# A two-block transformer step on one core: first transfers on one queue, first weights by quarters, eleven unread products in place of 28

## The chip, the cores and the metric

The kernel runs on one core of one Trainium2 chip. The metric is the device time of one execution in microseconds (us); lower is better. PE is TensorE, DVE is VectorE, ACT is ScalarE, POOL is GpSimd, SP is SyncE.

## The reference, cut to what matters

The reference takes 256 tokens of width 1024 (float32) through two blocks, each of two layers, with several kinds of attention, feed-forward parts and mixtures of experts. The very first step is the projection of the input `x` by the weights of the even mixer. The change touches how `x` and those weights come into the core, and the first products on them.

```python
def even_mixer(x, rel_bias, w_in, conv_w, a_log, dt_bias, norm_w, w_out):
    bsz, seq, _ = x.shape                 # 1, 256, width 1024
    q_a, k_a, v_a, z_a, b_a, a_a, q_b, k_b, v_b = jnp.split(x @ w_in, EVEN_SPLITS, axis=-1)
    ...
    o_b = dilated_attention(q_b.reshape(shp), k_b.reshape(shp), v_b.reshape(shp), rel_bias).astype(x.dtype)
    return jnp.concatenate([o_a, o_b], axis=-1) @ w_out
```

## The kernel before

Each engine has its own program, and waits on semaphores tie them together. `wait_ge` on an engine holds everything behind it on that engine, its DMA issues too. The work is an order written out by hand. Weights come in slots of 128 partitions x 4096 float32 (2 MB), by a list `LOADS`, into three slots (`ring`) that SP fills; SP waits for a slot's last reader (`used`) before it issues the next load into it. The list begins with `("we", 6)`, `("we", 7)`, `("we", 8)`, `("wev",)`, `("wev2",)`.

At the start two engines issue DMAs. SP issues all of `("we", 6)` in one DMA and then waits for `PAR`, the landing of three parameter transfers (`cp`, the rest of `kc`, `rp`), before `("we", 7)`. ACT issues, in this order, `x` half 0, the identity matrix `ident` (64 KB), `x` half 1, `cp`, the rest of `kc`, `rp`, and then begins its part of `even()`:

```python
for h in range(2):
    a.dma_start(x[:, h, :], ...).then_inc(s_x[h], 16)
    if h == 0:
        a.dma_start(ident, ins["kc"][:, 0:128]).then_inc(s_x[0], 16)
a.dma_start(cp[:, :], ins["cp"]).then_inc(s_par, 16)
```

PE (`even()` in `tensor`, line 925) first does 28 products on a tile of ones whose result nobody reads (`warm(28, ones)`). A float32 product shows in the trace as two MATMUL records. Then comes `first_tiles(0, ("we", 6), "qb")`, line 708. It transposes half 0 of `x` (`turn_x(0, 0)`: eight transposes into two PSUM banks, `kp` = 0 and 1), waits for all of `("we", 6)`, and multiplies. `part(c, h, kp)` is four products: column tile `c` (of 4), token half `h`, and four of the eight blocks of the inner dimension (`kp`). All four tiles of (h 0, kp 0) come first, then (h 0, kp 1) with the transposes of half 1 in the middle of them, then those of h 1: 64 products in all. The transposed `x` is copied out of PSUM into `xTs` by DVE for kp 0 and by ACT for kp 1 (`x_transposed`, lines 1577 and 2509); `ready(h, kp)` waits for that copy. After the first tiles PE waits for `PAR`, makes the product `hrow` and goes on with `("we", 7)` and `("we", 8)` in `proj_T`. DVE empties the four banks of the first tiles.

The weights lie in memory with the four column tiles side by side (`tiles`): element [k, c, n] at `512 k + 128 c + n` of a partition's row. For some weights (`NARROW`) the host lays them out tile by tile (`by_tile`): [c, k, n].

Of the kernel before, what the change touches and what calls it, by code (L numbers as in the profile page):

```python
# [215 lines left out]
CHUNKS = {4: SB_CH, 6: RET_CH}  # L216

NARROW = ("ws", "wso", "wr", "wrv", "wro")
LEVELS = (0, 1, 2, 4, 8, 16, 32, 64)


# [24 lines left out]
LOADS = all_loads()  # L246
# [41 lines left out]
PLACE = all_slots()  # L288
# [84 lines left out]
def emit(nc, ctx, ins, out):  # L373
# [8 lines left out]
    def sem(name):  # L382
        return ctx.enter_context(nc.semaphore(name))
# [22 lines left out]
    kc = sb("kc_sb", ncon)  # L406
# [20 lines left out]
    s_pe, s_dve, s_act, s_pool = sem("pe_done"), sem("dve_done"), sem("act_done"), sem("pool_done")  # L427

    s_x = [sem(f"x{h}_landed") for h in range(2)]
    s_par = sem("params_landed")  # L430
    s_ring = [sem(f"ring{i}_landed") for i in range(WIDE)]
    s_more = [sem(f"second{i}_landed") for i in range(WIDE)]
# [230 lines left out]
    def tensor():  # L663
# [44 lines left out]
        def first_tiles(n, src, tag, xT=xT):  # L708


            if src[0] in NARROW:
                view = slot(src, 32).rearrange("p (c k) n -> p k c n", c=4)
            else:
                view = slot(src, 8).rearrange("p k (c n) -> p k c n", c=4)

            def part(c, h, kp):
                tk = slice(h * 128, h * 128 + 128)
                for k in range(4 * kp, 4 * kp + 4):
                    r = mm(banks[c][:, tk], view[:, k, c, :], xT[:, k, tk], k == 0, k == 7)
                return r  # L720

            def ready(h, kp):
                t.wait_ge(*(v if kp == 0 and (n == 0 or h) else a)("xT", n, h, kp))

            turn_x(n, 0)
            if src[0] in NARROW:
                for h in range(2):
                    t.wait_ge(*half_arrived(src, h))
            else:
                t.wait_ge(*arrived(src))  # L730
            banks = [bank(tag, c) for c in range(4)]
            ready(0, 0)
            for c in range(4):
                part(c, 0, 0)
            ready(0, 1)
            for c in range(2):
                part(c, 0, 1)
            turn_x(n, 1)
            for c in range(2, 4):
                part(c, 0, 1)  # L740
            ready(1, 0)
            for c in range(4):
                part(c, 1, 0)
            ready(1, 1)
            for c in range(4):
                part(c, 1, 1).then_inc(s_pe, t.did(tag, c))
            t.note("used", src)

        def proj_T(src, tag, n, c, last):
            view = slot(src, 8)  # L750
            if c == 0:
                t.wait_ge(*arrived(src))
            b = bank(tag, n)
            for k in range(8):
                r = mm(b[:, 0:256], view[:, k, c * 128:c * 128 + 128], xT[:, k, :], k == 0, k == 7)
            r.then_inc(s_pe, t.did(tag, n))
            if c == last:
                t.note("used", src)
# [165 lines left out]

        def even():
            t.wait_ge(*g("ones"))
            warm(28, ones[:, :])
            first_tiles(0, ("we", 6), "qb")
            t.wait_ge(*PAR)
            t.wait_ge(*g("consts"))  # L930
# [1561 lines left out]
    def scalar():  # L2492
# [537 lines left out]
            tables("natural_log_exp_and_others")  # L3030
            a.note("pre", 6)

        for h in range(2):
            a.dma_start(x[:, h, :], ins["x"][h * 128:h * 128 + 128, :]).then_inc(s_x[h], 16)
            if h == 0:
                a.dma_start(ident, ins["kc"][:, 0:128]).then_inc(s_x[0], 16)
        a.dma_start(cp[:, :], ins["cp"]).then_inc(s_par, 16)
        a.dma_start(kc[:, 128:ncon], ins["kc"][:, 128:ncon]).then_inc(s_par, 16)
        a.dma_start(rp[:, :], ins["rp"].broadcast_to([128, nrow])).then_inc(s_par, 16)
# [167 lines left out]
    def sync():  # L3207
        def load_expert(name, src, h):

            i, _, old = PLACE[name]  # L3210
            lo = 2048 * h
            if i < SLOTS:
                dst = ring[:, i * 4096 + lo:i * 4096 + lo + 2048]
            else:
                dst = M[name[1]].ringx[:, (i - SLOTS) * 4096 + lo:(i - SLOTS) * 4096 + lo + 2048]
            if i >= SLOTS and (old is None or old[1] != name[1]) and i not in ABOVE[name[1]]:


                s.wait_ge(*(v("sbo", 15) if not name[1] else t("used", ("wro", 3)) if i == 3 else v("unit", 7)))
            elif i >= SLOTS and old is None:  # L3220

                for lane in (t, v, a, g):
                    s.wait_ge(*lane("pre", 3))
            elif old[0] in EXPERT:
                s.wait_ge(*t("used", old, h))
            else:
                s.wait_ge(*t("used", old))
            s.dma_start(dst, src[:, lo:lo + 2048]).then_inc((s_more if h else s_ring)[i], 16)

        def load_experts(names, src):  # L3230
            for h in range(2):
                for name in names:
                    load_expert(name, src(name), h)

        def last_used(name):

            return [p for p in LOADS[:LOADS.index(name)] if PLACE[p][0] == PLACE[name][0] and not (p[0] in ("mg", "mu", "md") and p[2] > 16)][-1]


        HEAD = (("wr", 0), ("wr", 1))  # L3240

        def load(name, src, old=None):
            i = PLACE[name][0]
            old = old or PLACE[name][2]
            if name[0] in NARROW:
                for h in range(2):
                    if old in FIRST:
                        n, first = FIRST[old]
                        s.wait_ge(*t("part", n, first + 2 * h + 1))
                    else:  # L3250
                        s.wait_ge(*(t("used", old) if ("used", old) in t.at else v("used", old)))
                    lo = 2048 * h
                    s.dma_start(ring[:, i * 4096 + lo:i * 4096 + lo + 2048], src[:, lo:lo + 2048]).then_inc(s_half[2 * i + h], 16)
                return
            if old is not None:
                s.wait_ge(*(t("used", old) if ("used", old) in t.at else v("used", old)))
            s.dma_start(ring[:, i * 4096:i * 4096 + width(name)], src).then_inc(s_ring[i], 16)

        def chosen(name):
            return ins[name[0]][bass.ds(ids[name[2] - 16] + name[1] * 16, 1)].rearrange("a p n -> (a p) n")  # L3260

        for place, name in enumerate(LOADS):
            if place == 1:
                s.wait_ge(*PAR)
            if name in HEAD:
                continue
            if name[0] not in EXPERT:
                load(name, source(name))
                continue
            if name[2] < 16:  # L3270

                before, behind = LOADS[place - 1], LOADS[place + 1]
                if name[2] % 2 and before == (name[0], name[1], name[2] - 1):
                    continue
                load_experts([name] + [behind] * (name[2] % 2 == 0 and behind == (name[0], name[1], name[2] + 1)), source)
                continue
            if name[0] != "mg" or name[2] not in (16, 17):
                continue
            l = name[1]
            n, m = 5 + 2 * l, M[l]  # L3280
            if name[2] == 16:
                s.wait_ge(*v("eids", n, 0))
                ids = [s.e.value_load(m.eids[0:1, 0:1], min_val=0, max_val=15)]
                for w in EXPERT:
                    load_experts([(w, l, 16)], chosen)
                continue
            s.wait_ge(*v("eids", n, 6))
            ids += [s.e.value_load(m.eids[0:1, j:j + 1], min_val=0, max_val=15) for j in range(1, 7)]
            flag = s.e.value_load(m.eids[0:1, 7:8], min_val=0, max_val=1)
            seen, rest = dict(s.seen), moe_loads(l, 9, 12)  # L3290
            with s.e.If(flag > 0):
                for i in range(0, len(rest), 2):
                    load_experts(rest[i:i + 2], chosen)
                if l == 0:
                    for name in HEAD:
                        load(name, source(name))
            with s.e.Else():
                for i in range(WIDE):
                    mine = [PLACE[name][1] for name in rest if PLACE[name][0] == i]
                    s.e.wait_ge(s_ring[i], 16 * (mine[0] - 1))  # L3300
                    s.e.sem_inc(s_ring[i], 16 * len(mine))
                    s.e.wait_ge(s_more[i], 16 * (SECOND[[name for name in rest if PLACE[name][0] == i][0]] - 1))
                    s.e.sem_inc(s_more[i], 16 * len(mine))
                s.seen = dict(seen)
                if l == 0:

                    for name in HEAD:
                        load(name, source(name), last_used(name))
            s.seen = seen
# [128 lines left out]
```

## Time and profile before

| | us |
|---|---|
| median of 3 runs | 1819.53 |
| lowest and highest | 1815.80 and 1820.54 |
| the profiled execution, its own time | 1823.21 |
| its span | 1821.5 |
| its mean granted TensorE clock | 0.982 of full |

PE is busy for 1736.7 us of the span (95%), DVE for 976.5 us, ACT for 641.2 us, POOL for 230.2 us; the DMA engines move 443.05 MB, 243 GB/s in the mean. All times in the rows further down are from that profiled execution, counted from the start of the span. A row of the timeline merges instructions of one kind; a bracket behind it tells how long the engine sat idle before and what ended that.

### The profile page before, as it was taken

Reading aid. Unit: us, or ns where it says so; the run is one execution under the profiler, and the core shown is the slowest. Engines: PE = TensorE matmul, PEld = TensorE weight load, DVE = VectorE, ACT = ScalarE, POOL = GpSimd, SP = SyncE. Lnnn points to the kernel's source line nnn. Section 1 sums busy time; section 2 is a strip of 40 time slices with the busy share of each in tenths; the row PEclk is TensorE's granted clock in tenths of the full one; section 3 lists DMA queues with packets and bytes.
Section 4 is the critical chain, followed back from the end, with each engine's and each line's share of the span. In section 5 each row is a group of like instructions: output and inputs, shape, how many; then the busy total and the mean of one; then the engine's idle time right before and its main releaser. Section 6 shows DMA issues by size and latency. Waiting matters only on the chain. (4 is left out here: it accounts for less than half of the span.)

```text
span 1821.5 us, 25863 instructions
## 1 busy us (share of the span) xinstructions
PE 1736.7 (95%) x10464; PEld 1280.2 (70%) x10464; DVE 976.5 (54%) x1806; ACT 641.2 (35%) x1078; POOL 230.2 (13%) x217
## 2 busy tenths in 40 slices
PE   9999999999999989999999989999899999899987
PEld 8788875799886544999888764434489898544434
DVE  1176664688541575787456663233267867533223
ACT  1025322467430224666446431111144455311111
POOL 0000000163110130353002302000000200010000
PEclk9899999999999889999999999999999999999999
DMA  8422186445434595455344659999934555799995
GB/s 306 149 94 93 60 339 249 185 181 213 162 139 162 185 362 232 161 213 187 139 144 177 247 202 420 420 420 420 371 121 160 185 208 208 308 419 420 420 420 230
DMA packets 51853, 443.05 MB, mean 243 GB/s; under 512 B 5900, under 2 KB 6160, under 8 KB 9104
## 3 DMA queue, kind: packets, MB, share of 16 engines
q1 hardware_dynamic: 47664, 426.79, 60.1%
q0 software_dynamic: 2480, 8.92, 1.3%
q10 hardware_dynamic: 1584, 5.61, 0.8%
q8 instruction: 86, 1.41, 0.3%
q14 instruction: 39, 0.32, 0.0%
HBM read 440.25 MB, written 1.05 MB: 242 GB/s over the span
## 5 line engine op out<-in xcount | busy, mean ns | idle before, releaser
L88 ACT ACTIVATE arena<-ps 128x384 f32<-128x384 f32 (+5 forms) x233 | 101.6, 436 | 546.3 <-PE ps L82 344.1
L82 PE MATMUL ps<-ringx,arena 128*64 128x512 f32 x1056 | 276.2, 594 | 7.9 <-DMA ringx<-in_mg 3.5
L82 PE MATMUL ps<-xsplit_f,wsplit_f 128*128 128x256 f32 x2112 | 257.1, 284 | 3.5 <-ACT xsplit_f L88 2.7
L82 PEld LDWEIGHTS ps<-xsplit_f,wsplit_f 128*128 128x128 f32 x2112 | 255.5, 193 | 5.5 <-ACT xsplit_f L88 4.2
L82 PE MATMUL ps<-ring,arena 128*64 128x512 f32 (+1 forms) x704 | 228.8, 598 | 9.5 <-DMA ring<-in_mu 6.0
L91 DVE TENSOR_TENSOR wsplit_f<-ring,wsplit_f 128x1024 fp32r<-128x1024 f32 x132 | 180.6, 1372 | 70.4 <-ACT wsplit_f L88 70.4
L82 PEld LDWEIGHTS ps<-ringx,arena 128*64 128x64 f32 x1056 | 89.6, 137 | 170.3 <-issue 156.3
L82 PE MATMUL ps<-xTs,ring 128*128 128x256 f32 (+1 forms) x960 | 188.3, 356 | 2.3 <-ACT xTs L88 1.8
L82 PEld LDWEIGHTS ps<-xTs,ring 128*128 128x128 f32 x960 | 163.0, 193 | 24.5 <-issue 6.6
L88 ACT ACTIVATE wsplit_f<-ring 128x1024 fp32r<-128x1024 f32 x132 | 138.2, 1051 | 57.5 <-PE ps L82 56.5
L82 PEld LDWEIGHTS ps<-ring,arena 128*64 128x64 f32 (+1 forms) x704 | 78.6, 148 | 104.8 <-issue 89.2
L91 DVE TENSOR_TENSOR ringlo<-ring,ringhi 128x1024 fp32r<-128x1024 f32 x88 | 120.7, 1387 | 58.1 <-ACT ringhi L88 57.7
L82 PE MATMUL ps<-arena 128*128 128x128 f32 (+5 forms) x1128 | 142.2, 306 | 4.2 <-DVE arena L91 2.0
L91 POOL TENSOR_TENSOR small<-small,half 128x1 f32<-128x1 f32 x16 | 9.3, 583 | 1031.3 <-DVE small L95 1029.7
L82 PEld LDWEIGHTS ps<-arena 128*128 128x128 f32 (+2 forms) x1128 | 127.5, 192 | 16.5 <-DVE arena L91 4.0
L99 DVE SCALAR_TENSOR_TENSOR arena<-ps,cp_sb,arena 128x255 f32<-128x255 f32 (+2 forms) x230 | 110.9, 482 | 45.7 <-ACT arena L88 34.2
L91 DVE TENSOR_TENSOR arena<-arena,ps 128x384 f32<-128x384 f32 (+2 forms) x74 | 42.9, 579 | 165.6 <-PE ps L82 152.8
L82 PE MATMUL ps<-wsplit_f,gsplit 128*128 128x512 f32 x528 | 120.1, 389 | 0.0
L82 PEld LDWEIGHTS ps<-wsplit_f,gsplit 128*128 128x128 f32 x528 | 99.0, 188 | 20.5
L88 ACT ACTIVATE ringhi<-ring 128x1024 fp32r<-128x1024 f32 x88 | 91.7, 1052 | 52.9 <-PE ps L82 45.2
L91 POOL TENSOR_TENSOR arena<-arena 128x256 f32<-128x256 f32 (+1 forms) x58 | 78.3, 1350 | 196.4 <-DVE arena L91 110.3
L82 PE MATMUL ps<-xth,ringhi 128*128 128x256 f32 x320 | 94.9, 296 | 2.2 <-DVE ringlo L91 1.7
(197 smaller groups left out, 2425.0 us busy)
## 6 DMA issues: line engine op xcount, KB each, us to landing
ring<-in_ada SPq DMA_DIRECT2D x24, 2048.0 KB, 8.0
ring<-in_wu SPq DMA_DIRECT2D x22, 2048.0 KB, 8.1
ringx<-in_mg SPq DMA_DIRECT2D x44, 1024.0 KB, 20.8
ringx<-in_mu SPq DMA_DIRECT2D x44, 1024.0 KB, 23.8
ringx<-in_md SPq DMA_DIRECT2D x44, 1024.0 KB, 26.1
ring<-in_md SPq DMA_DIRECT2D x24, 1024.0 KB, 25.5
ring<-in_mg SPq DMA_DIRECT2D x24, 1024.0 KB, 20.7
ring<-in_mu SPq DMA_DIRECT2D x24, 1024.0 KB, 23.9
```

Of the source, the lines that this page charges most:

```text
L82: return self.e.matmul(o, l, r, start=start, stop=stop, skip_group_check=True)
L88: return self.e.activation(o, i, f, **k)
L91: return self.e.tensor_tensor(o, a, b, op)
L99: return self.e.scalar_tensor_tensor(out=o, in0=a, scalar=s, in1=b, op0=op0, op1=op1)
```

## The change

Four things change. (1) SP issues `x` half 0, `ident`, quarter 0 of `("we", 6)`, `x` half 1 and the quarters 1 to 3, each quarter (512 KB, one column tile) with a semaphore of its own. It then issues `("we", 7)` at once, and waits for `PAR` before `("we", 8)`. (2) ACT issues nothing until half 1 of `x` has landed; then it issues `cp`, `kc` and `rp`. (3) The 28 unread products become 11, and three more follow the transposes of half 0. (4) For n = 0, `first_tiles` goes tile by tile: tiles 0 and 1 for half 0 (both kp), each as its quarter lands, with the transposes of half 1 between them; then half 1 of each tile, tiles 2 and 3 with both halves. The host lays out all `we` weights tile by tile, and `proj_T` reads them so; the number and the shapes of products are the same.

```diff
@@ first_tiles @@
-            if src[0] in NARROW:
+            if src[0] in BY_TILE:                    # BY_TILE = NARROW + ("we",)
                 view = slot(src, 32).rearrange("p (c k) n -> p k c n", c=4)
...
-            else:
+            elif n:
                 t.wait_ge(*arrived(src))
+            if n == 0:
+                warm(3, ones[:, :])
             banks = [bank(tag, c) for c in range(4)]
+            if n == 0:
+                for c in range(2):
+                    t.wait_ge(s_tile[c], 16)
+                    for kp in range(2):
+                        ready(0, kp)
+                        part(c, 0, kp)
+                    if c == 0:
+                        turn_x(n, 1)
+                for c in range(4):
+                    if c >= 2:
+                        t.wait_ge(*((s_tile[c], 16) if c < 3 else arrived(src)))
+                        part(c, 0, 0)
+                        part(c, 0, 1)
+                    for kp in range(2):
+                        ready(1, kp)
+                        r = part(c, 1, kp)
+                    r.then_inc(s_pe, t.did(tag, c))
+                t.note("used", src)
+                return
@@ proj_T @@
-            view = slot(src, 8)
+            if src[0] in BY_TILE:
+                view = slot(src, 32)[:, 8 * c:8 * c + 8, :]
+            else:
+                view = slot(src, 8)[:, :, c * 128:c * 128 + 128]
...
-                r = mm(b[:, 0:256], view[:, k, c * 128:c * 128 + 128], xT[:, k, :], k == 0, k == 7)
+                r = mm(b[:, 0:256], view[:, k, :], xT[:, k, :], k == 0, k == 7)
@@ even (PE) @@
-            warm(28, ones[:, :])
+            warm(11, ones[:, :])
@@ scalar @@
-        for h in range(2):
-            a.dma_start(x[:, h, :], ins["x"][h * 128:h * 128 + 128, :]).then_inc(s_x[h], 16)
-            if h == 0:
-                a.dma_start(ident, ins["kc"][:, 0:128]).then_inc(s_x[0], 16)
+        a.wait_ge(s_x[1], 16)
         a.dma_start(cp[:, :], ins["cp"]).then_inc(s_par, 16)
@@ sync @@
+        def load_x(h):
+            s.dma_start(x[:, h, :], ins["x"][h * 128:h * 128 + 128, :]).then_inc(s_x[h], 16)
+
+        def load_first(c):
+            lo, name = 1024 * c, LOADS[0]
+            s.dma_start(slot(name, 1)[:, 0, lo:lo + 1024], source(name)[:, lo:lo + 1024]) \
+                .then_inc(s_tile[c] if c < 3 else s_ring[PLACE[name][0]], 16)
+
+        load_x(0)
+        s.dma_start(ident, ins["kc"][:, 0:128]).then_inc(s_x[0], 16)
+        load_first(0)
+        load_x(1)
+        for c in range(1, 4):
+            load_first(c)
         for place, name in enumerate(LOADS):
-            if place == 1:
+            if place == 0:
+                continue
+            if place == 2:
                 s.wait_ge(*PAR)
```

## Rows read from the trace of the kernel before

**Rows 1.** The page of the profile: its span.
```profile
span 1821.5 us, 25863 instructions
```

**Rows 2.** The timeline, 0 to 28 us: start, length, engine, line, operation, count, idle before.
```profile
...
1.07 7.99 PE L82 MATMUL ps<-ones 128*128 128x128 f32 x56 [1.07 <-POOL ones L114]
...
2.23 0.53 ACTq L117 DMA_DIRECT2D cp_sb<-in_cp  x1
...
3.28 0.49 ACTq L117 DMA_DIRECT2D rp_sb<-in_rp  x1
...
10.75 1.09 PE L85 MATMUL ps<-kc_sb,xs 128*128 128x128 f32 x8 [1.69 <-DMA kc_sb<-in_kc]
11.45 0.69 DVE L102 COPY xTs<-ps 128x512 f32<-128x512 f32 x1 [10.12 <-PE ps L85]
11.93 1.28 ACT L88 ACT_TABLE_LOAD   x1 [11.93 <-PE ps L85]
...
12.28 5.60 PE L82 MATMUL ps<-xTs,ring 128*128 128x128 f32 x48 [0.44 <-DVE xTs L102]
13.23 0.60 ACT L88 ACTIVATE xTs<-ps 128x512 f32<-128x512 f32 x1
...
17.72 1.04 PE L85 MATMUL ps<-kc_sb,xs 128*128 128x128 f32 x8
...
18.59 9.10 PE L82 MATMUL ps<-xTs,ring 128*128 128x128 f32 x80
...
27.62 0.81 PE L82 MATMUL ps<-kc_sb,cp_sb 32*4 32x384 f32 x2
```

**Rows 3.** The timeline from 16 us, the DMA queue of SP.
```profile
...
17.30 0.82 SPq L117 DMA_DIRECT2D ring<-in_we  x2
```

**Rows 4.** Windows from the start and one later: busy times, PEclk, DMA share, GB/s.
```profile
...
0.00:4.10 4.10, 3.03 (x14) 3.03 (x15) 0.24 (x4) 0.00 (x0) 0.60 (x7) 1.00 0.51 133
...
0.00:6.70 6.70, 5.63 (x37) 5.63 (x38) 0.24 (x4) 0.00 (x0) 0.60 (x7) 1.00 0.72 251
0.00:16.00 16.00, 12.80 (x97) 12.41 (x98) 0.93 (x5) 1.88 (x2) 0.60 (x7) 1.00 0.87 342
20.00:24.00 4.00, 4.00 (x38) 4.00 (x38) 0.00 (x0) 2.18 (x3) 0.00 (x0) 1.00 0.94 401
```

**Rows 5.** DMA view, 0 to 8 us: GB/s in 40 slices of 0.2 us, then queues.
```profile
...
GB/s 0 0 0 0 0 0 0 0 0 492 573 82 0 82 20 82 348 369 492 123 307 696 532 123 369 881 266 102 410 860 266 123 451 799 266 143 676 717 184 123
...
q1 hardware_dynamic: 109, 1.79, 61.3%
q10 hardware_dynamic: 99, 0.41, 13.9%
```

**Rows 6.** Windows around waits of PE: PE busy (instructions), PEclk, DMA share, GB/s.
```profile
...
79.30:92.90 13.60, 13.60 (x44) 0.50 0.30 127
...
528.40:530.40 2.00, 0.16 (x2) 1.00 0.00 0
...
666.70:670.80 4.10, 0.38 (x8) 0.88 1.02 436
670.80:676.60 5.80, 5.45 (x30) 0.50 0.98 414
1316.10:1318.80 2.70, 0.18 (x2) 0.91 0.99 413
1318.80:1321.70 2.90, 2.90 (x7) 0.50 0.10 34
1325.90:1329.20 3.30, 0.10 (x2) 0.90 0.64 257
1329.20:1332.00 2.80, 2.80 (x13) 0.50 0.01 3
```

**Rows 7.** Groups of instructions on PE, 1 to 4 us: busy, mean ns.
```profile
...
L82 PE MATMUL ps<-ones 128*128 128x128 f32 x13 | 3.1, 433 | 1.1 <-POOL ones L114 1.1
```

**Rows 8.** The same groups, 5 to 8 us.
```profile
...
L82 PE MATMUL ps<-ones 128*128 128x128 f32 x29 | 3.4, 275 | 0.0
```

More of the change, by code:

```diff
@@ L218 @@
 NARROW = ("ws", "wso", "wr", "wrv", "wro")
+BY_TILE = NARROW + ("we",)
 LEVELS = (0, 1, 2, 4, 8, 16, 32, 64)
@@ L429, in emit @@
     s_x = [sem(f"x{h}_landed") for h in range(2)]
+    s_tile = [sem(f"first_tile{c}_landed") for c in range(3)]
     s_par = sem("params_landed")
@@ L3372 @@
     ins = {"x": a["x"][0]}
-    ins["we"] = tiles(_np.concatenate([we[:, 0:3072], we[:, 3084:4620]], 1), 8, 512)
+    even_tiles = tiles(_np.concatenate([we[:, 0:3072], we[:, 3084:4620]], 1), 8, 512)
     ins["wev"] = tiles(we[:, 4620:5132], 8, 512)
@@ L3390, in by_tile @@
         return w.reshape(-1, 128, 8, 4, 128).transpose(0, 1, 3, 2, 4).reshape(w.shape)
+    ins["we"] = by_tile(even_tiles)
     ws = a["sb_w_in_2"][0]
```

## The prediction

> **What bounds the kernel now.** I read the page first: the kernel is long, with a span of 1821.5 us [rows 1], and PE is busy for nearly all of it. So what the first 28 us save or lose on PE is carried through to the end: every later load waits for a slot that PE frees, and so moves along with PE. The timeline of the first 28 us comes next [rows 2]. The reader is to see a chain there. PE's 28 unread products run from 1.07 to 9.06. Then PE waits 1.69 us for the `x` half 0 and the identity, and starts the transposes at 10.75. DVE's copy of the first bank ends at 12.14, and the products on `("we", 6)` start at 12.28. ACT's copy of the second bank is ready at 13.83 (13.23 and 0.60), but the 16 products of kp 0 hide it. From 12.28 on PE has no idle time until `hrow` at 27.62. So the start is bound by the landing of `x`, then by PE. SP issues the next weights only at 17.30, when the last parameter transfer has landed [rows 3]; the windows and the DMA view tell how the bytes come in [rows 4, 5]. Last, I looked for what a wait of PE does to its clock [rows 6 to 8].
>
> The sum is made on the moment at which `hrow` starts, 27.62 in the profiled execution (span 1821.5 us, own time 1823.21 us). The median of the runs, 1819.53 us, is 3.7 us below that own time; I subtract the same difference from both.
>
> **When the first bytes land.** All bytes of the start (x 1.05 MB, identity 0.07, `("we", 6)` 2.10, parameters 2.27: 5.4 MB with roundings) are moved by 16.0 (342 GB/s x 16.0 us = 5.5 MB) [rows 4], and SP's wait for the last of them ends at 17.30 [rows 3]. So a landing comes some 1.3 us behind its last byte. After the change the order is one queue's. x half 0 and the identity are 590 KB; 545 KB are moved by 4.1 us (133 x 4.1) and 1682 KB by 6.7 us (251 x 6.7) [rows 4]. So 590 KB are there at 4.2 and land at 5.5. Quarter 0 makes it 1114 KB, at 5.4, landing 6.7. x half 1 makes it 1638 KB, at 6.6, landing 7.9. In the first 8 us two queues shared evenly by packets, 109 to 99, which is why 16 KB packets of weights held back the 4 KB packets of `x`; per byte both kinds took the same (61.3% of 16 x 8 us for 1.79 MB, 13.9% for 0.41 MB: 23 GB/s of an engine each) [rows 5]. So smaller packets cost nothing here.
>
> **PE until the wait.** Eleven unread products are 22 records. By 4.0 us 13 had run at 433 ns each, later ones have 275 ns [rows 7, 8], so the 22 end at about 5.0, before `x` lands: removing 17 products costs nothing and removes nothing from the path. Transposes 5.5 to 6.6 (1.09). DVE's copy is ready at 5.5 + 0.70 (10.75 to 11.45) + 0.69 = 6.9. The three new products (6 records at 9.10/80 = 0.114 us) end at 7.2 and cover that copy. part(0, 0, 0), eight records, ends at 8.1 [rows 2].
>
> **The new wait.** Now PE needs ACT's copy of kp 1. ACT waits for half 1 of `x` (7.9), and three issues are queued behind that wait: before, they took from 2.23 to 3.28 + 0.49 = 3.77, so 1.54 us. Only then does it come to the table load and the copy, 11.93 to 13.83, so 1.90 us [rows 2]. The table load began only after the transposes, so it sits behind that wait and isn't done ahead. The copy is ready at 7.9 + 1.54 + 1.90 = 11.3, and PE goes on at 11.4. PE idles for 3.3 us where before it had 12 more products of kp 0 to do.
>
> The row shows the copy starting 1.30 us after the load began, with nothing behind the load. The Trainium skill (ScalarE: Activation LUTs, What ACT_TABLE_LOAD costs) puts 1.38 us of drain beside a load of 1.28 us; by it the copy would be ready 1.4 us later and the forecast 1.4 us higher. I go by the row.
>
> **The rest of the first tiles.** 60 products are 120 records x 0.114 = 13.65 us, the transposes of half 1 put 18.59 - 17.72 = 0.87 us among them [rows 2]. 11.4 + 13.65 + 0.87 = 25.9, against 27.62: a gain of 1.7 us. Quarters 1 to 3 are 3.2 MB with all before them. Even if `cp` takes half of the bandwidth from 8.9 on, quarter 1 is there by 11 and quarter 3 by 18, and they are needed after 13 and after 21. Their waits cost nothing. The other layout leaves shape and count of all products alone: 0. `("we", 7)` goes earlier, which nothing needs, and can only delay the parameters: 5.47 MB were moved by 16.0, the 2.0 MB left over take 5.0 us at 401 GB/s [rows 4], so all parameters land by 22.3, 3.6 us before PE asks for them. `("we", 8)`, 5 us later than before, is needed some 12 us after `hrow`: hidden.
>
> **The clock.** Three other waits show what follows. Over 4.1 us with 0.38 us of work, over 2.7 and over 3.3 us, the granted clock fell in each, and PE went on at 0.50, the lower level of 1.2 GHz, for 5.8, 2.9 and 2.8 us. A wait of 2.0 us at 528 left it at 1.00 [rows 6]. The new wait of 3.3 us is like the three. A stretch at half speed costs half of its length: 2.9, 1.5 or 1.4 us, 1.9 in the mean, and the bounds are 0 and that of the longest low stretch shown, 13.6 us at 79.3 [rows 6], 6.8 us. I take 1.9, by the three nearest rows. (If the clock has not yet risen at 5 us with fewer unread products, the loss up to 11.4 lies in the wait, and what comes after is the same price.)
>
> Sum: -1.7 + 1.9 = +0.2 us. Median 1819.7 us; profiled execution 1823.4, span 1821.7.
>
> **The rivals.**
> (a) The clock holds over the wait. Then the gain of 1.7 us stays: 1817.8. For it: the wait at 528 [rows 6], and that PE has 0.9 us of products right before. Against it: three of three at 2.7 us and more.
> (b) The bytes come sooner on one queue. From 2.2 to 3.0 us nearly nothing moved [rows 5]; without that dip all landings are 0.8 us earlier, the copy is ready at 10.5 and the end is 25.1: 2.5 us gained before the clock's price, 1818.9 with it, 1817.0 without. The Trainium skill (DMA: Bandwidth & Descriptors, Anatomy of one DMA) gives, for the software path, a fixed 2.0 us and 436 GB/s; by that estimate x half 1 would be there at 6.6. The rows here speak for 7.9.
> (c) ACT isn't late, because the table load or the issues lie beside the wait after all. Then products run without a stop from 7.2: 7.2 + 128 x 0.114 + 0.87 = 22.6, just after the parameters' 22.3. That is 5.0 us gained, 1814.5, and the most that this change can give. Against it: the table load at 11.93 came 0.09 us behind the transposes, not at the start [rows 2].
> (d) The other side: the clock stays low through most of the first tiles. From 3.4 us at the lower level on, the kernel is slower than before; at 13.6 us, as at 79.3 [rows 6], it loses 6.8 - 1.7 = 5.1 us: 1824.6; beyond 14.4 us it is slower by 0.3%. Against it: with the same products the clock held all the way from 12.28 before, and the three stretches after waits were 5.8 us at most.
> (e) The change moves nothing at all, as the end of the first tiles stays within 0.5 us of 27.6: that is the forecast's own result, by two terms that cancel, and the trace tells them apart.
>
> **How the numbers follow.** Forecast 0.57, with its own range 1818.3 to 1821.2 (price of the clock 1.4 to 2.9, landings by 0.8 us sooner or 0.5 later). (a) and (b) 0.28 together, (c) 0.09, (d) 0.06. A change under 0.3% (5.5 us) can't be told from none here: the three runs of before lie 4.7 us apart. Only (c) with luck, or (d) with more than its row, gets past it: faster 0.03, slower 0.03, the same 0.94. The range leaves out (d) and most of (c) and takes in the scatter of a median of a few runs, some 1.5 us: 1815.5 to 1822.5.
>
> **What would show it.** In the profile after: transposes at about 5.5; a wait of PE for ACT's `xTs` copy of about 3.3 us, ending near 11.4; ACT's issues at 7.9 to 9.4 and its table load right behind; MATMUL records of some 433 ns in place of 275 after that wait for 3 to 6 us; `hrow` near 27.8; `("we", 7)` issued before 5 us. The forecast is wrong if PE doesn't wait for ACT, if x half 1 lands before 7 us or after 9 us, if the records after the wait keep 275 ns, or if PE waits for parameters at `hrow`.

## The result, and the profile after

| | us |
|---|---|
| before, median of 10 runs | 1818.95 (1815.80 to 1823.61) |
| after, median of 10 runs | 1825.95 (1821.16 to 1827.46) |
| ratio | 1.0032, interval 1.0019 to 1.0045 |
| profiled execution after | 1826.19, span 1824.5 |

The change makes the kernel slower by 0.32%, some 6 us (the two medians themselves lie 7.0 us apart). The forecast was 1819.7 with a range up to 1822.5: the time lies 3.5 us above it.

The timeline of the changed kernel from the start (start, length, engine, line, what, count, idle before); it answers to [rows 2, 3]:

```profile
0.81 0.39 SPq L117 DMA_DIRECT2D xs<-in_x  x1
...
5.93 1.70 PE L85 MATMUL ps<-kc_sb,xs 128*128 128x128 f32 x8
...
8.23 1.16 PE L82 MATMUL ps<-xTs,ring 128*128 128x128 f32 x8
9.51 0.38 ACTq L117 DMA_DIRECT2D cp_sb<-in_cp  x1
9.93 0.45 ACTq L117 DMA_DIRECT2D kc_sb<-in_kc  x1
10.40 0.45 ACTq L117 DMA_DIRECT2D rp_sb<-in_rp  x1
10.95 1.28 ACT L88 ACT_TABLE_LOAD   x1 [10.95 <-issue]
12.24 0.60 ACT L88 ACTIVATE xTs<-ps 128x512 f32<-128x512 f32 x1
...
12.89 1.16 PE L82 MATMUL ps<-xTs,ring 128*128 128x128 f32 x8 [3.51 <-ACT xTs L88]
...
13.89 1.70 PE L85 MATMUL ps<-kc_sb,xs 128*128 128x128 f32 x8
...
15.38 13.69 PE L82 MATMUL ps<-xTs,ring 128*128 128x128 f32 x112
...
24.19 0.21 ACT L88 ACTIVATE small<-cp_sb 128x8 f32<-128x8 f32 x1 [6.67 <-DMA rp_sb<-in_rp]
...
29.00 0.80 PE L82 MATMUL ps<-kc_sb,cp_sb 32*4 32x384 f32 x2
```

The reader sees the forecast chain, link by link: `x` half 1 lands at 9.5 and releases ACT's issues; then comes the table load, then the copy, which ends at 12.84, and PE has waited 3.51 us. Behind it the transposes take 1.70 us in place of 1.04. `hrow` starts at 29.00, 1.4 us later than before [rows 2].

Windows of the changed kernel (PE, PEld, DVE, ACT, POOL busy, then granted clock, DMA share, GB/s), to compare with [rows 4, 6]:

```profile
0.00:6.70 6.70, 5.63 (x26) 5.63 (x27) 0.24 (x4) 0.00 (x0) 0.60 (x7) 1.00 0.69 195
...
12.80:17.50 4.70, 4.61 (x26) 4.61 (x27) 0.69 (x1) 1.90 (x3) 0.00 (x0) 0.64 0.98 414
```

After the wait the granted clock is 0.64 in the mean up to 17.5 us. By 6.7 us only 1.31 MB are there (195 x 6.7) and not 1.68. The DMA queues from 0 to 8 us (packets, MB, share of 16 engines):

```profile
q1 hardware_dynamic: 574, 1.66, 71.2%
```

But 1.4 us at `hrow` are not 3.0 us in the span, nor 6 in the median. Farther on the two profiles run together again: the first product on the output weights starts at 300.01 after and at 299.57 before. The rest appears at one place. The timeline of PE in the changed kernel there:

```profile
682.84 0.22 PE L82 MATMUL ps<-tmpn,gate 128*32 128x4 f32 x8
686.26 3.44 PE L82 MATMUL ps<-ring,gate 128*32 128x512 f32 x16 [3.20 <-DMA ring<-in_ada]
689.46 0.31 PE L82 MATMUL ps<-tmpn,gate 128*32 128x4 f32 x8
689.70 2.09 PE L82 MATMUL ps<-arena,ones 128*128 128x512 f32 x4
```

And in the kernel before:

```profile
683.00 0.22 PE L82 MATMUL ps<-tmpn,gate 128*32 128x4 f32 x8
685.05 1.92 PE L82 MATMUL ps<-ring,gate 128*32 128x512 f32 x16 [1.83 <-DMA ring<-in_ada]
686.79 0.22 PE L82 MATMUL ps<-tmpn,gate 128*32 128x4 f32 x8
```

PE comes to the same load at the same time (within 0.2 us), waits 3.20 us in place of 1.83, and then runs 16 records in 3.44 us in place of 1.92: the clock has fallen after the longer wait (granted 0.57 in the mean from 686 to 690 us). The next step begins at 689.70 against 686.94. Most of these 2.8 us stay: the spans end 3.0 us apart. So there were two losses: one at the start, which the forecast had, and one at 683 us, which it had not. The DMA view of the moment at which SP issues that load, 677 us, first before (677.2 to 678.0), with its time to landing:

```profile
q8 instruction: 1, 0.02, 8.3%
...
ring<-in_ada SPq DMA_DIRECT2D x1, 2048.0 KB, 7.6
```

and after (677.0 to 678.0, and the queues at 683.2 to 684.8):

```profile
ring<-in_ada SPq DMA_DIRECT2D x1, 2048.0 KB, 9.0
...
q1 hardware_dynamic: 57, 0.69, 102.7%
q8 instruction: 1, 0.02, 3.7%
```

The same 2 MB take 9.0 us in place of 7.6. A packet of the instruction queue (16 KB, 0.95 us) starts at 683.7 after, 6.5 us behind the load's issue and just as its last bytes come in; before, it started at 677.3, with the issue. A load raises its semaphore in 16 steps. After, the trace has 15 of them 7.4 us behind the issue and the last alone at 9.0; before, 15 were in by 7.5 and the last came at 7.6. So one sixteenth of the load is late, and the rest is not.

### The profile page after: what moved, and what is told of

Its sections match the earlier page's. It is cut to its first block and busy times, and to the rows that moved or that the text cites. A ratio compares the mean times of both kernels' runs of the same rounds, so it can differ in the third digit from the quotient of the medians.

```text
span 1824.5 us, 25810 instructions
## 1 busy us (share of the span) xinstructions
PE 1736.2 (95%) x10436; PEld 1280.3 (70%) x10436; DVE 976.6 (54%) x1806; ACT 641.1 (35%) x1078; POOL 229.5 (13%) x217
```

## The experiments

Each time is a median; each ratio is against the kernel before, measured alongside, with a 95% interval. Theory 1: the loss is ACT's late copy and the low clock behind it. Theory 2: the layout or the early load costs farther on. Theory 3, formed on the first profiles: the length of PE's program ahead of a place sets where the instruction packets fall among the loads. The change takes 14 products out of that program; the trace has 28 matmul and 28 weight-load instructions of PE less for them, 56 in all. Theory 4: chance.

**The changed kernel again.** No edit.

> The changed kernel once more, unaltered, for a second profile. In the first one hrow starts at 29.00 us, 1.4 us later than before, and 1.6 us more come at 683 us, where PE waits for an ada load and its clock then falls. Theory 1 (the loss is ACT's late copy and the low clock after it, and what lies behind it is the luck of the clock): hrow again at 28 to 31, the wait of 3.5 us again, median 1822 to 1827, and the place of the later differences need not be the same. Theory 2 (something else in the change, the layout of the weights or the early load, costs further on): the same 1.6 us again at 683 us.

1824.96 us, ratio 1.0022 (1.0009 to 1.0035). `hrow` at 29.04 after a wait of 3.48 us; at 682 us a wait of 3.50 us, and the clock falls again. Both losses come back. Theory 4 would have the second one come and go.

**ACT copies first.**

```diff
 def x_transposed(...):                  # scalar
     for h in range(2):
+        if h and n == 0:
+            load_params()                # a.wait_ge(s_x[1], 16) and the three issues
```

> ACT copies half 0 of x before it waits for half 1 and issues the parameters; all else as in the changed kernel. Theory 1: no wait of PE for ACT of over 1 us, no low clock in the first tiles; their 64 products run from 8.2 to about 23.7, hrow waits for the parameters until about 24.5; so 4.5 us under the changed kernel and 2 to 3 us under the kernel before, 1814 to 1818. Theory 2 (the loss lies in the layout or behind the start): still 1822 or more.

1819.42 us, ratio 0.9988 (0.9974 to 1.0002). Its timeline of the start:

```profile
9.02 0.60 ACT L88 ACTIVATE xTs<-ps 128x512 f32<-128x512 f32 x1
9.50 0.38 ACTq L117 DMA_DIRECT2D cp_sb<-in_cp  x1
...
9.67 1.16 PE L82 MATMUL ps<-xTs,ring 128*128 128x128 f32 x8 [0.29 <-ACT xTs L88]
...
11.54 12.67 PE L82 MATMUL ps<-xTs,ring 128*128 128x128 f32 x112
...
25.29 0.80 PE L82 MATMUL ps<-kc_sb,cp_sb 32*4 32x384 f32 x2 [1.08 <-DMA rp_sb<-in_rp]
```

The wait is 0.29 us, 112 records take 12.67 us in place of 13.69, and `hrow`, now held by the parameters, starts 3.7 us earlier than in the changed kernel. The start is won, 2.3 us under before; the wait at 680 us is 3.44 us with a fall of the clock, as in the changed kernel. The ratio is 2.2 us under before (4.7 under to 0.4 over), as expected (2 to 3 us); the expected 1814 to 1818 itself was missed, as the kernel before stood at 1820.89 here. By the profile 2.3 us won and 2.8 lost should leave 0.5 us over, at the edge of the interval: in this time the second loss doesn't show.

**Unread products in the wait.**

```diff
+                        if (c, kp) == (0, 1):
+                            warm(15, ones[:, :])
                         ready(0, kp)
```

> 15 unread products are put into PE's wait for ACT's copy; the wait itself stays as long. Theory 1: MATMUL records after it keep 275 ns, first tiles end 1.7 us earlier than in the changed kernel, hrow at 27.3; median 1.5 to 3 us lower, 1822 to 1824. If the clock at the start has no price: no change, hrow at 29.0.

1819.09 us, ratio 0.9996 (0.9983 to 1.001). Its timeline of PE at the start:

```profile
8.37 3.51 PE L82 MATMUL ps<-ones 128*128 128x128 f32 x30
12.05 1.16 PE L82 MATMUL ps<-xTs,ring 128*128 128x128 f32 x8 [0.17 <-ACT xTs L88]
13.05 1.04 PE L85 MATMUL ps<-kc_sb,xs 128*128 128x128 f32 x8
13.92 12.67 PE L82 MATMUL ps<-xTs,ring 128*128 128x128 f32 x112
26.52 0.81 PE L82 MATMUL ps<-kc_sb,cp_sb 32*4 32x384 f32 x2
```

ACT comes behind its three issues as in the changed kernel, yet the transposes take 1.04 us again and `hrow` starts at 26.52, 2.5 us sooner. Two things make up the 2.5 us. `x` half 1 landed 0.8 us sooner in this profile (8.7 in place of 9.5), which is no work of the edit. And from PE's going on to `hrow` it is 14.47 us here (12.05 to 26.52) and 16.11 us in the changed kernel (12.89 to 29.00): the low clock cost 1.6 us. The ratio lies 5 us under that of the changed kernel, more than the 1.5 to 3 us expected; the wait at 675 us is 2.0 us. It has 29 unread products, not 14, and this gave theory 3.

**The layout alone.** The kernel before with `BY_TILE`, the host's `by_tile` and the new view in `proj_T`.

> The kernel before with one part of the change alone: the even weights laid out tile by tile and read so. Theory 1: the same as before within 0.1%, hrow at 27.6. Theory 2 (the layout costs): 3 to 6 us slower, with longer records of the products on xTs and ring.

1818.29 us, ratio 0.9994 (0.9979 to 1.0008), `hrow` at 27.64. Theory 2 falls for the layout; the early load of `("we", 7)` has no run of its own.

**The kernel before again.**

> The kernel before, unaltered, for a second profile. So far PE waits at about 683 us for an ada load: 1.8 us in before, 2.0 and 2.2 us in the two experiments that have 28 or 29 unread products at the start, and 3.2, 3.5 and 3.4 us in the three kernels that have 14; in those three a 16 KB packet of the instruction queue starts 0 to 1 us before the load's first landing. Theory 3 (the count of PE's instructions ahead of it sets where the instruction packets fall among the loads): again 1.8 to 2.2 us here, an instruction packet near 677, no low clock at 685. Theory 4 (it is chance): 3.2 us or more is as likely here. Time within 0.1% of before.

1820.61 us, ratio 1.0 (0.9987 to 1.0012). Wait of 2.02 us at 681 us, no fall.

**The count alone.** The kernel before, with the same PE time in half the instructions.

```diff
-            warm(28, ones[:, :])
+            wide(14)        # mm(b[:, 0:256], ones, ones[:, 0:1] broadcast to 256 columns)
```

> The kernel before with 14 unread products of 256 columns in place of 28 of 128: the same time of PE, hrow at 27.6, but 14 products fewer, as many as the change takes out in all. Theory 3: the wait at 683 us is 3.2 to 3.5 us and the clock falls after it, so some 3 us slower than before, 1821 to 1825. Theory 4, and theory 1 alone: 1.8 to 2.2 us as in before, no change.

1822.73 us, ratio 1.0015 (1.0004 to 1.0027). Its timeline at the start and at the load:

```profile
27.61 0.80 PE L82 MATMUL ps<-kc_sb,cp_sb 32*4 32x384 f32 x2
...
685.44 3.58 PE L82 MATMUL ps<-ring,gate 128*32 128x512 f32 x16 [3.66 <-DMA ring<-in_ada]
```

And the load's issue in the DMA view of e4, with its time to landing, and the queues at the load's end (682.0 to 683.6):

```profile
ring<-in_ada SPq DMA_DIRECT2D x1, 2048.0 KB, 9.4
...
q8 instruction: 1, 0.02, 3.7%
```

`hrow` starts to 0.01 us as before; the whole loss at 683 us is there. This is theory 3 without any other part of the change: 2.8 us (0.7 to 4.9). Its products are 256 columns wide, so the width differs too, but PE is at its first transposes at 10.75 in both.

**The length restored.** In the changed kernel, by slow products and then by no work at all.

```diff
                         if (c, kp) == (0, 1):
+                            tiny(14)     # e5: mm(b[:, 0:2], ones, ones[:, 0:2])
+                            for _ in range(112): t.e.wait_ge(s_x[0], 32)     # e11, in its place
```

> The changed kernel with 14 unread products of two columns in PE's wait for ACT: the count of before, but hardly any work, and the wait as long. Theory 3: the wait at 683 us is back to 1.8 to 2.2 us and 3 us of the loss are gone, 1820 to 1823, with hrow still at 28.5 to 29.5. Theory 1 alone: as the changed kernel, 1824 to 1826.

> The changed kernel with 112 waits on a semaphore that has long been reached (56 instructions) in PE's wait for ACT: PE's program has the length of before again, and PE does no work for it. Theory 3: hrow at 29.0 to 29.5 and the low clock at the start as in the changed kernel; the load that PE waits for at 683 us has its last landing 0.7 to 1.5 us behind the first (not 2.2 to 2.5), the wait is 2.5 us at most; 1821 to 1823, 2 to 3 us under the changed kernel. If the program's length doesn't matter and only PE's work did in e2_fill_wait: 3.2 us or more at 683 us and 1824 to 1826.

e5: 1822.52 us, ratio 1.0014 (1.0001 to 1.0027); the load takes 8.3 us, the wait is 2.54 us and not the 1.8 to 2.2 expected, and the clock falls nonetheless. e11: 1824.72 us, ratio 1.002 (1.0008 to 1.0032), above what was expected. Its page counts 25,866 instructions against 25,810 in the changed kernel, so the 56 are there. The time misses, but the load and the wait come out as theory 3 has them. The load in its DMA view (679.0 to 680.0), with the instruction packet and the time to landing:

```profile
q8 instruction: 1, 0.02, 6.7%
...
ring<-in_ada SPq DMA_DIRECT2D x1, 2048.0 KB, 7.7
```

and PE's timeline of e11 behind the wait:

```profile
686.99 1.93 PE L82 MATMUL ps<-ring,gate 128*32 128x512 f32 x16 [1.91 <-DMA ring<-in_ada]
```

The loss at 683 us is gone to the last tenth in this profile. But the 56 instructions took longer than the wait that was to hide them: ACT's copy was ready at 12.2, PE went on at 13.45, the clock was low behind it, and `hrow` started at 30.82, 1.8 us later than in the changed kernel. So the total hardly moved.

**ACT first, with the length restored behind the first tiles.** `tiny(14)` in e6, the 112 waits in e12, ahead of the wait for `PAR`.

> ACT copies half 0 first (as in e1_act_copies_first), and 14 unread products of two columns run behind the first tiles, in the wait for the parameters. Theories 1 and 3 together: hrow at about 25.3 and the short wait at 683 us: 2.3 us under before, 1815 to 1818, and 3 us under e1_act_copies_first. Theory 1 alone: as e1_act_copies_first.

> As e1_act_copies_first, with the same 56 instructions of waits behind the first tiles, where PE waits for the parameters anyway. hrow at 24 to 27 by how long the instructions take; the wait at 680 us 1.8 to 2.5 us. By theories 1 and 3 1.5 to 4 us under before, 1815.5 to 1818. If e6_act_first_tiny lost its gain to something other than its slow products: no gain here either.

Both were expected to win and lost: 1822.49 us, 1.0018 (1.0006 to 1.0031), and 1822.59 us, 1.0012 (1.0 to 1.0023). The wait at 680 us was 1.8 and 2.05 us with no fall, as theory 3 has it; the times, which were also forecast by it, missed by 4 to 6 us. In e12 the waits took 3.98 us, `hrow` started at 27.47, and the window behind it (PE busy, granted clock, DMA share, GB/s) shows the new loss:

```profile
27.40:32.70 5.30, 5.23 (x11) 0.50 0.99 420
```

That is 2.6 us lost at half speed, which with 27.47 for 27.62 is near its 2.2 us. In e6 the 28 records of two columns took 3.19 us and the profiled run shows no fall behind them. In the mean its runs lost 32.5 us to the clock, those of the kernel before beside them 28.8; but where, I can't show.

**More of them.** 42 products of 84 columns in the kernel before.

> The kernel before with 42 unread products of 84 columns in place of 28 of 128: about the same time of PE at the start, 14 products more. Theory 3: the instruction packets come earlier among the loads than in before, the one at 677 us some 5 us sooner, in the load ahead; the wait at 683 us stays 1.8 to 2.2 us and the time that of before, within 0.1%. If any other count than 28 is bad, or the start's products matter in another way: slower, as in e4_half_the_count.

1828.68 us, ratio 1.0056 (1.0042 to 1.0071): a badly made experiment. A record of 84 columns took 0.22 us, no less than one of 128 at the lower clock, the 84 records ran until 19.3, and `hrow` started at 36.8. The wait at the load was 2.2 us, and the clock fell behind it. Theory 3 had the instruction packet some 5 us sooner with 56 instructions more; it came 0.4 us behind the load's issue. That forecast missed: the packet's place is no plain shift by the count.

**The wait at 293 us filled, too.** PE waits there for the first output weights in every profile. In e7 14 unread products run in that wait, which also gives PE's program its old length from there on; e9 adds sooner parameters; e10 has them in the kernel before, with `wide(14)` at the start.

```diff
+            warm(14, ones[:, :])
             t.wait_ge(*arrived(("woe", 1)))
```

> ACT copies half 0 first, and 14 unread products of 128 columns fill PE's wait for the first woe load at about 293 us, so that from there on PE's instruction count is that of before. Theories 1 and 3: hrow at 25.3; the clock keeps its upper level at 294 us (6.8 us of low clock go, 3 us); the wait at 680 us is 1.8 to 2.2 us with no fall after it. 1813 to 1817 in all, 4 to 6 us under before. If only the start counts: 1819, as e1_act_copies_first.

> The fastest version so far once more, for its time: 5 runs were few, and it was picked from several. If it holds, 5 to 8 us under before, hrow at 23.8 to 25.3, no low clock at 293 us, and at most 2.5 us of wait at 673 us. If it was luck of the clock: 3 us under before or less.

> As e7_act_first_fill_woe, and ACT issues the parameters right behind its first copy without waiting for half 1 of x, and SP waits for them before the second weights. Parameters land near 18, hrow starts at 24.2 with no wait, the second weights land at about 25 and cost up to 1 us of wait behind it. 0 to 1 us under e7_act_first_fill_woe, 1813 to 1816. If the sharing of the queues holds back half 1 of x or the quarters: hrow later than 25.3 and no gain.

> The kernel before with 14 unread products of 256 columns at the start and 14 of 128 columns in the wait for the first woe load: the count of before from 294 us on. Filling alone: the clock keeps its upper level after the wait and 1.7 to 3.4 us go, 1816 to 1818; the wait at 683 us is 1.8 to 2.2 us, where e4_half_the_count, which has the same start, had 3.7 us. If the start's count and not the count ahead of the loads matters: the wait at 683 us is 3.2 us or more again.

e7: 1813.31 us (5 runs), ratio 0.9964 (0.995 to 0.9977), and again 1814.09 us (12 runs), 0.9969 (0.9955 to 0.9982): it beats both kernels, before by 6 us and after by some 11. The timeline of PE at the place, in the second of its profiles:

```profile
293.53 3.39 PE L82 MATMUL ps<-ones 128*128 128x128 f32 x28
296.98 3.27 PE L82 MATMUL ps<-ring,arena 128*128 128x512 f32 x7
```

and the window there (PE busy, granted clock, DMA share, GB/s):

```profile
295.00:300.00 5.00, 4.94 (x25) 1.00 0.90 357
```

Seven records take 3.27 us there; in the changed kernel PE waited 4.23 us, the seven took 5.35 us, and the window behind was at half speed, in the same columns:

```profile
300.00:304.20 4.20, 4.18 (x5) 0.50 0.66 281
```

e9: 1819.15 us, 0.9991 (0.998 to 1.0002). `hrow` started at 24.23 with no wait, but then PE waited 2.91 us for the second weights, with a fall of the clock: the early issue of `("we", 7)` is needed once the start is fast. e10: 1816.99 us, 0.9989 (0.9976 to 1.0002): its wait at 676 us is 2.15 us where e4 had 3.66, as expected, but the clock fell behind it all the same. In the first tiles its clock was low too, which e4 with the same start doesn't show, and `hrow` came at 29.8.

**Across all profiles.** The load that SP issues at 668 to 682 us, the instruction packet nearest to it, and the wait. Two values stand for a profile and its repetition:

| kernel | PE instructions ahead, against before | packet after the load's issue | issue to landing | wait of PE | clock falls |
|---|---|---|---|---|---|
| before, again | 0 | -0.2, -0.6 | 7.6, 7.8 | 1.8, 2.0 | no, no |
| e2, e3, e6, e11, e12 | 0 (e2: +4) | -0.3 to 0.3 | 7.6 to 8.0 | 1.8 to 2.2 | no |
| e7, again | 0 | 0.0, -0.2 | 8.2, 7.6 | 2.4, 1.3 | no, no |
| e5 | 0 | -0.4 | 8.3 | 2.5 | yes |
| e9, e10 | 0 | 1.5, 1.4 | 8.5, 8.5 | 2.2, 2.2 | yes, yes |
| e8 | +56 | 0.4 | 8.6 | 2.2 | yes |
| after, again | -56 | 6.5, 6.8 | 9.0, 9.3 | 3.2, 3.5 | yes, yes |
| e1 | -56 | 6.8 | 9.3 | 3.4 | yes |
| e4 | -56 | 6.3 | 9.4 | 3.7 | yes |

The four profiles with 56 instructions less stand apart in packet, landing and wait, and in them the last of the load's 16 steps comes 1.6 to 1.7 us behind the 15th; elsewhere it is at most 0.8. But e9 and e10, with the old count, have the packet 1.5 us into the load, and they, e5 and e8 land at 8.3 to 8.6 with a fall. The old count alone doesn't keep the clock up. The trace doesn't name whose instructions a packet carries; that they are PE's is inferred from e4 and e11, where PE's count alone moved the packet.

And what the clock took, as the mean over the runs of span x (1 - granted clock): before 29.4 us (35 runs), after 33.4 (10) and 33.4 (12), e1 29.5, e2 28.6, e4 30.8, e6 32.5, e7 24.3 and 24.5. What is left of the span is 1789.4 before, 1790.1 and 1789.3 after. Each mean of 10 or 12 runs is good to some 1 us. So in the runs the loss of the changed kernel is time at the lower clock, 4 us of it, and so is most of e7's gain; the 1.4 us that the load took longer in the profiles can't be told from the noise in what is left.

## Why the prediction was wrong

- **The start** was right in kind and close in size. Terms with what they measured: PE's wait 3.3 us, measured 3.5, ended by ACT's copy as forecast. The clock's price 1.9 us, measured 1.6. `hrow` forecast at 27.8, measured 29.0. The difference is the landing of `x` half 1, 7.9 forecast and 9.5 measured, less 0.3 us of the clock's price. That price was 1.6 us in both profiles of the changed kernel; in e5 and e11 it was 2.9 us (17.3 and 17.4 us from PE's going on to `hrow`).
- **The step mis-sized there** is "So smaller packets cost nothing here". In the first 8 us after, 574 packets moved 1.66 MB in 71.2% of the engines' time, 18 GB/s of an engine, where 16 KB and 4 KB packets side by side had 23 [rows 5]. The bytes come later, and `x` half 1 with them: between 8.7 and 9.6 in ten profiles with this order. That the size of the packets is the reason isn't shown: the 4 KB packets of before had 23 as well, and in the changed kernel packets of at most 4 KB had 25 from 8.0 to 9.5 us (393 GB/s over 16 engines). Packet size and the one queue changed together, and no run parts them. The parameters landed at 24.2 and not at 22.3, still hidden.
- **PE's start** was forecast wrong on both sides, without effect here. `x` half 0 and the identity had landed by 4.6, not 5.5; but the 22 unread records ran until 5.9, not 5.0, as they kept to some 0.22 us each. So the unread products held PE, and not `x`. The wait for ACT hid it.
- **The step that failed** is "removing 17 products costs nothing and removes nothing from the path", with its like, that what PE does behind `hrow` is carried through unchanged. The start's instructions (14 products fewer in all, as three were added) are also bytes that the same DMA engines fetch. With 56 instructions less, the packet that fell on the issue of a load at 677 us fell on that load's end, the load took 1.4 us longer, and the clock fell behind the wait. e4 shows it alone (2.8 us), e11 takes it away at its place.
- **The sum** of the two places is 1.4 us at `hrow` and 2.8 us at the load, 4.2 us (the two spans lie 3.0 us apart, as the profile of before lost more at 80 us); the runs show 6 and 4 us in two measurements (intervals 3.5 to 8.2 and 1.6 to 6.4).
- **Rivals.** (a), a clock that holds, and (b), sooner bytes, were both wrong. (c), ACT in time, is what e1 made, and it was worth 3.7 us at `hrow`, held by the parameters. (d) named the clock, but at the start, and asked for 14 us of it there; 2.8 of the 4.2 us came from a wait 650 us farther on. That the measured time lies near the 1824.6 of (d) is chance.
- **The chances** put 0.03 on slower by over 0.3%. The bound "the most that this change can give" held for gains; for losses nothing bounded it, as PE has some thirty waits of over 0.9 us behind the start, and whether the clock falls behind one can change with the edit.

Open: where e6's other runs lose their time; why a packet of 0.95 us holds the last step of a load back by 1.6; what besides the count sets a packet's place (e8, e9, e10); and how much of a difference between two measurements is chance. One kernel's profiles differ at 80 us: in the changed kernel the granted clock from 78 to 93 us was 0.66 in one and 0.89 in the other, 3.4 us of time, in work that was the same.

## What to carry to other kernels

After removing or adding instructions on the busiest engine, look at where the instruction packets fall among the loads that it waits for: the effect can lie far from the edit. Price a wait of TensorE by what the clock takes behind it, and try unread full-width products in it; they kept the clock up in e2 (start) and in e7 and e10 (293 us). Two-column products in e5 and bare waits in e11 and e12 didn't. When transfers move off an engine that also computes, see what stands behind its new wait: here one copy of 0.6 us should have gone first.

## What the runs showed of the hardware

- A 16 KB instruction packet (0.95 us on one of the 16 engines) at the end of a 2 MB load went with a landing at 9.0 to 9.4 us, 1.4 to 1.8 us later than the 7.6 of before. Within 0.6 us of the load's issue, the landing was at 7.6 to 8.3 us (8.6 in e8).
- 56 instructions of waits that were already met took 3.98 us on PE in e12, 71 ns each, and 4.92 us in e11, 88 ns each. A float32 record of 2 columns took 0.11 us at the upper clock, as long as one of 128.
- 1.8 to 2.2 us of waiting at the load left the clock up in seven profiles; in e8, e9 and e10 it fell after 2.2 us, and in e7 it held after 2.4 us. From 2.5 us on it fell in all.
- At the start records run at half the later rate though the profile's granted clock reads 1.00: 22 unread records took 5.06 us in the changed kernel and 4.25 us in e6, whose start is the same, so the moment at which the rate rises differs from profile to profile.
